# Hybrid flow-matching step on one core: VectorE's side work in the recurrent mixer regrouped, its output double-buffered, and the output projections split into fp32r

## The reference

```
out = jnp.concatenate([c_out, d_out], axis=-1) @ w_out       # (384, 1024) @ (1024, 1024)
x = x + gate * out
```

```
sa = einsum(s, kk_t)
s  = s * w_t - sa (kk_t * a_t) + v_t k_t
o  = einsum(s, r_t)
```

## Time and profile before

| | us |
|---|---|
| median of 3 runs (lowest, highest) | 1813.3 (1811.26, 1814.56) |
| the profiled execution, its own time | 1816.77 |
| span of the profile | 1815.1 |
| PE busy | 1563.8 (86%) |
| PEld busy | 1229.5 (68%) |
| DVE busy | 1128.4 (62%) |
| ACT busy | 723.6 (40%) |
| POOL busy | 265.4 (15%) |

### The profile page before, as it was taken

The page is one execution under the profiler, slowest core; times in us unless marked ns, Lnnn a source line. Parts: engine busy times, 40 slices in busy tenths (PEclk is TensorE's granted clock), DMA queues, the critical chain, the costliest instruction groups (busy, mean ns, idle before and its releaser), DMA issues. The chain is left out here.

```text
span 1815.1 us, 33539 instructions
## 1 busy us (share of the span) xinstructions
PE 1563.8 (86%) x13261; PEld 1229.5 (68%) x13261; DVE 1128.4 (62%) x1495; ACT 723.6 (40%) x1101; POOL 265.4 (15%) x276
## 2 busy tenths in 40 slices
PE   4779989799999987789898888868589999999982
PEld 1456665399999974476676767753468888888871
DVE  1158761279877612585856767641268889888884
ACT  3112222242332311441423415210267777877763
POOL 3400000142222110011101021001100111111111
PEclk8898997899999967899998989879589999999996
DMA  8794543088766204111010000020668999999984
GB/s 306 222 315 139 177 137 92 4 260 262 252 205 201 93 1 130 53 30 39 8 44 24 23 5 3 4 81 20 265 266 338 385 378 372 369 369 370 370 318 164
DMA packets 157576, 321.96 MB, mean 177 GB/s; under 512 B 13187, under 2 KB 104661, under 8 KB 151317
## 3 DMA queue, kind: packets, MB, share of 16 engines
q1 hardware_dynamic: 129750, 201.32, 31.0%
q0 software_dynamic: 26416, 114.28, 18.4%
q10 hardware_dynamic: 1296, 4.72, 0.6%
HBM read 299.15 MB, written 24.25 MB: 178 GB/s over the span
## 5 line engine op out<-in xcount | busy, mean ns | idle before, releaser
L2657 DVE TENSOR_TENSOR gate_up_low<-expert_gate_up,gate_up_high 128x1408 fp32r<-128x1408 f32 x147 | 231.5, 1622 | 17.9 <-ACT gate_up_high L2579 17.7
L2579 ACT ACTIVATE gate_up_high<-expert_gate_up 128x1408 fp32r<-128x1408 f32 x147 | 197.7, 1374 | 29.4 <-PE banks L2475 20.6
L2473 PE MATMUL banks<-gate_up_high,gathered_high 128*128 128x512 f32 (+1 forms) x432 | 165.9, 384 | 9.2 <-DVE gate_up_low L2657 9.2
L2475 PE MATMUL banks<-gate_up_high,gathered_low 128*128 128x512 f32 (+1 forms) x432 | 163.7, 379 | 0.0
L2474 PE MATMUL banks<-gate_up_low,gathered_high 128*128 128x512 f32 (+1 forms) x432 | 163.4, 378 | 0.0
L2653 DVE TENSOR_TENSOR down_low<-expert_down,down_high 128x1024 fp32r<-128x1024 f32 x99 | 118.7, 1223 | 51.5 <-ACT down_high L2572 51.2
L2572 ACT ACTIVATE down_high<-expert_down 128x1024 fp32r<-128x1024 f32 x99 | 102.2, 1052 | 75.6 <-PE banks L2475 61.2
L1137 DVE SCALAR_TENSOR_TENSOR mod_sums<-next_mod_w,silu_cond,mod_sums 128x2048 f32<-128x2048 f32 x48 | 125.4, 2659 | 7.0 <-DMA mod_sums<-in_mod_b 7.0
L1013 PE MATMUL banks<-ffn_in_high,gate_up_w_high 128*128 128x384 f32 x352 | 118.8, 337 | 5.0 <-DVE ffn_in_low L1118 4.1
L1015 PE MATMUL banks<-ffn_in_high,gate_up_w_low 128*128 128x384 f32 x352 | 118.4, 336 | 0.0
L1014 PE MATMUL banks<-ffn_in_low,gate_up_w_high 128*128 128x384 f32 x352 | 118.3, 336 | 0.0
(11 more groups left out here) (379 smaller groups left out, 3247.4 us busy)
## 6 DMA issues: line engine op xcount, KB each, us to landing
expert_gate_up<-in_moe_w_up SPq DMA_DIRECT2D x76, 704.0 KB, 8.0
expert_gate_up<-in_moe_w_gate SPq DMA_DIRECT2D x76, 704.0 KB, 7.8
expert_down<-in_moe_w_down POOLq DMA_DIRECT2D x99, 512.0 KB, 5.6
next_mod_w<-in_mod_w POOLq DMA_DIRECT2D x24, 1024.0 KB, 5.2
late_w<-in_mod_w POOLq DMA_DIRECT2D x16, 1024.0 KB, 5.2
gate_up_w<-in_ffn_w_gate SPq DMA_DIRECT2D x22, 512.0 KB, 6.1
gate_up_w<-in_ffn_w_up SPq DMA_DIRECT2D x22, 512.0 KB, 5.7
normed_by_channel<-in_ffn_w_down SPq DMA_DIRECT2D x22, 512.0 KB, 6.5
```

The source lines that it names most:

```text
L2473: nc.tensor.matmul(out, a[0], b[0], start=first, stop=False)
L2475: return nc.tensor.matmul(out, a[1], b[0], start=False, stop=last)
L2579: nc.scalar.activation(WH[:, u % SPLIT, :], raw[:, u % RAW, :], ACT.Copy).then_inc(high, 1)
L2657: v.tensor_tensor(WL[:, u % SPLIT, :], raw[:, u % RAW, :], WH[:, u % SPLIT, :], ALU.subtract).then_inc(low, 1)
```

## The change

Two functions are edited, and they have nothing to do with each other.

In `rwkv`, VectorE's side work gets other places. The log sums, `after_own` and one half of the reciprocal of `key_norm` move between the `xm` and the `up` step of a level; `out_norm` and `finished` move behind the chain; `keys` move behind the last level, and the four products of `operands` and the three steps of `shifted_values` into the gaps of the chain. The addition into `scan_out` now comes ahead of the masks of the first tile of pair j+1. `scan_out` gets two buffers, and ScalarE waits for pair j-2 in place of j-1.

In `mixed`, k becomes the outer loop: for each k ScalarE rounds one row block of weights (128 by 1024) and one of inputs (128 by 384), VectorE takes the differences, and TensorE runs 18 fp32r matmuls (3 for each of the 6 units). All six units end in the pass of the last k. The gated result goes through 2 buffers, the space of the first weight block, in place of 6.

```diff
 def mixed(R, l, ahead):
...
-        Y = sb(f"gated{l}", [P, 6, BANK])
-        done, gated = R.sem(f"mixed_done{l}"), R.sem(f"mixed_gated{l}")
+        MH, ML = sb(f"mixed_high{l}", [P, OUT_SPLIT, TOK], F32R), sb(f"mixed_low{l}", [P, OUT_SPLIT, TOK], F32R)
+        Y = W[:, 0, :].rearrange("p (u n) -> p u n", u=2)
+        WH, WL = sb(f"w_out_high{l}", [P, OUT_SPLIT, D], F32R), sb(f"w_out_low{l}", [P, OUT_SPLIT, D], F32R)
...
             def _(pe):
-                for t in range(TT):
-                    for h in range(2):
-                        for k in range(KT):
-                            if t == 0 and h == 0 and k % 2 == 0:
-                                pe.wait_ge(loaded[k // 2], 16)
-                            mm = nc.tensor.matmul(R.B[2 * t + h][:, :], R.MT[:, k, t * P:(t + 1) * P], W[:, k, h * BANK:(h + 1) * BANK],
-                                                  start=(k == 0), stop=(k == KT - 1))
-                        mm.then_inc(done, 1)
+                for k in range(KT):
+                    s = k % OUT_SPLIT
+                    pe.wait_ge(w_low, k + 1)
+                    pe.wait_ge(m_low, k + 1)
+                    for u, (t, h) in enumerate(units):
+                        tok, cols = slice(t * P, (t + 1) * P), slice(h * BANK, (h + 1) * BANK)
+                        nc.tensor.matmul(R.B[u][:, :], MH[:, s, tok], WH[:, s, cols], start=(k == 0), stop=False)
+                        nc.tensor.matmul(R.B[u][:, :], MH[:, s, tok], WL[:, s, cols], start=False, stop=False)
+                        mm = nc.tensor.matmul(R.B[u][:, :], ML[:, s, tok], WH[:, s, cols], start=False, stop=(k == KT - 1))
...
             def _(act):
+                for k in range(KT):
+                    act.wait_ge(loaded[k // 2], 16)
+                    if k >= OUT_SPLIT:
+                        act.wait_ge(w_used, k - OUT_SPLIT + 1)
+                    nc.scalar.activation(WH[:, k % OUT_SPLIT, :], W[:, k, :], ACT.Copy).then_inc(w_high, 1)
+                    nc.scalar.activation(MH[:, k % OUT_SPLIT, :], R.MT[:, k, :], ACT.Copy).then_inc(m_high, 1)
...
             def _(dve):
+                for k in range(KT):
+                    dve.wait_ge(w_high, k + 1)
+                    nc.vector.tensor_tensor(WL[:, k % OUT_SPLIT, :], W[:, k, :], WH[:, k % OUT_SPLIT, :], ALU.subtract).then_inc(w_low, 1)
+                    dve.wait_ge(m_high, k + 1)
+                    nc.vector.tensor_tensor(ML[:, k % OUT_SPLIT, :], R.MT[:, k, :], MH[:, k % OUT_SPLIT, :], ALU.subtract).then_inc(m_low, 1)
+                for u, (t, h) in enumerate(units):
                     dve.wait_ge(done, u + 1)
+                    if u >= 2:
+                        dve.wait_ge(added, u - 1)
...
 def rwkv(R):
...
-                    if j:
-                        act.wait_ge(dve_done, dve_at(f"yn.{j - 1}"))
+                    if j >= 2:
+                        act.wait_ge(dve_done, dve_at(f"yn.{j - 2}"))
...
+                def in_level(l, x, j):
+                    if (l, x) == (0, "up"):
+                        log_sum(j, 0)
+                    elif (l, x) == (1, "xm"):
+                        log_sum(j, 1)
+                    elif (l, x) == (1, "up"):
+                        before_own(j)
+                    elif (l, x) == (2, "xm"):
+                        after_own(j)
+                    elif (l, x) == (2, "up"):
+                        backward(j)
+                    elif l == 3:
+                        key_norm(j, 0 if x == "xm" else 1)
+                    elif (l, x) == (4, "up"):
+                        keys(j)
...
+                def between(gap, j):
+                    if gap == 1:
+                        operand(j, 0)
+                        operand(j, 1)
+                    elif gap in (2, 3):
+                        operand(j, gap)
+                    elif 4 <= gap < 7:
+                        shifted_values(j, gap - 4)
...
                     chains(j)
-                    if more:
-                        shifted_values(j + 1)
-                        first_inverse(0, j + 1)
+                    if j:
+                        out_norm(j - 1)
+                        finished(j - 1)
                     dve.wait_ge(pe_done, pe_at(f"out.{j}"))
                     dve.wait_ge(act_done, act_at(f"vu.{j}"))
-                    v.tensor_tensor(OS[:, :], OS[:, :], B[6][:, 0:TOK], ALU.add).then_inc(dve_done, dve_inc(f"os.{j}"))
+                    v.tensor_tensor(OSs[:, j % 2, :], OSs[:, j % 2, :], B[6][:, 0:TOK], ALU.add).then_inc(dve_done, dve_inc(f"os.{j}"))
+                    if more:
+                        first_inverse(0, j + 1)
                     dve.wait_ge(pe_done, pe_at(f"mean.{j}"))
```

152 lines of the change are left out of this document (85 added, 67 removed).

## The result

The changed kernel takes **1768.6 us** (median of 4 runs, 1765.4 to 1770.1), the kernel before on the same chip 1812.3 (4 runs, 1809.6 to 1814.6): a ratio of 0.9757, 95% interval 0.9737 to 0.9778, or 43.7 us less. The forecast was 1774.4, the range 1761 to 1791. The profiled execution after took 1765.4 us with a span of 1763.4, where 1815.1 stood before.

A forecast was written before the change was run, and what follows sets the result against it. It took the scan as bound by hand-overs between engines and what delays them, the projections by TensorE's work. 33.2 - 7.7 + 7.5 + 5.9 = 38.9 us off 1813.3 gave 1774.4 us, range 1761 to 1791.

The forecast's parts named there:

- One sign of being wrong: Projections: the prediction called itself wrong if fp32r products were spaced by more than 0.23 us past the first 3 us.
- Levels: The scan's levels, six pairs: VectorE's side work moved under waits gains 33.2 us, at 29.4 us per pair with side work.
- 0.9 (`after_own`, now between the two steps): Level 2: `after_own` between masked product and additions costs its whole 0.9 us, within 5.1 for the level.
- The 0.2 for hand-overs: Levels: an allowance of 0.2 us for hand-overs within the 29.4 us of each pair with side work.
- Chain: From the first u step on: the products and shifted v moved there cost 7.7 us, 3.0 plus 4.7 in pair 4.
- The delay of 1.5 in pair 0: Chain of pair 0: `beta` and `k_grown`, 2.8 us, in a wait of 1.30 for the second u step delay it 1.5.
- the cover of 2.32: Chains of pairs 1 to 3: a 2.32 us wait for the second u step covers `beta` and `k_grown`, leaving 0.5 each.
- Behind the chain: Behind the chain: adding into `scan_out` ahead of the masks gains 1.5 us in each of pairs 0 to 4, 7.5 in all.
- Projections: The two output projections: splitting them by k gains 1.7 us in layer 0 and 4.2 in layer 1, 5.9 in all.
- the full collision with GpSimd: Chain: GpSimd's work holds `beta` and `k_grown` to 2.57 us each, 11.7 more in five pairs, 1786 us; chance 0.17.
- a clock that falls in the levels: Levels: idle TensorE drops its clock, 2.4 us per level; all 25 give 1834, chance 0.04; a few 1780 to 1794, 0.10.
- The rule of the Trainium skill: Chain: the VectorE and GpSimd port lock makes `beta` and `k_grown` wait for GpSimd operations; gain some 3.5 us smaller, 1778.

The follow-up runs named there:

- waits_only: The changed kernel with the levels' side work one slot earlier, so nothing stands between the two steps of levels 2 and 3: 1762.6 us.
- masks_first: The changed kernel with the first tile's masks and inverse back ahead of the addition into `scan_out`: 1775.8 us.
- spread_out: The changed kernel with side work one slot earlier, chain products spread singly, the shifted v behind `finished` and 32 idle ScalarE activations per projection: 1753.6 us.
- gpsimd_later: The changed kernel with GpSimd's turn started behind the last of the chain's four products, in place of behind `neg_kk_a`: 1764.4 us.
- products_ahead: The changed kernel with the chain's four products back between `keys` and the first u step: 1794.5 us.

## Why the prediction was right, and where its sizes were off

The mechanism of the main term was right: time was lost where VectorE's side work stood between hand-overs, and comes back where it stands under waits. Most of the signs came: level 2 to the first u step 16.5 us ("near 17"), `beta` and `k_grown` 2.70 together (2.8), the projections 42.3 and 42.7, the last addition 8.2 behind the first gated product. One sign of being wrong came as well: fp32r products were spaced by more than 0.23 us past the first 3 us. That the total was within 5 us is in part luck. The scan gave 11.6 us more than its terms, the projections and the experts 7.5 less, and these two misses cancel in the main. Term by term:

- **Levels, 37.5 for 33.2.** The step "0.9 (`after_own`, now between the two steps)" and the same for 1.3 of the reciprocal counted whole lengths; a part is given back by the additions behind them, and `waits_only` measured 1.4 for the two in place of 2.2. The 0.2 for hand-overs was not needed either. That is 0.9 a pair, all of the difference in pairs 0 to 4. The halves of the reciprocal took 1.34 and 1.35, as assumed (1.3).
- **Chain, +4.0 for +7.7.** The delay of 1.5 in pair 0 came out as 1.39, but by another sum. Where the prediction put it, between the first s step and the second u step, it is 1.10. The first s step is 0.76 later, a term that the prediction doesn't have: before, VectorE came to the first u step so late that the s step followed at once (the row below, behind the u step at 823.15), and now it waits for TensorE (947.05 above has that wait in pair 2). Behind the second u step 0.47 is won back. In pairs 1 to 3 the step that failed is the cover of 2.32: that wait stood in a chain whose granted clock had fallen to 0.50, and with the clock at 1.00 it went away. At the full clock the cover is pair 0's 1.30; the delay is 1.4 there too, and the clock gives back 1.6 (15.23 for 13.65). The prediction had the clock as a risk of the levels and did not look for it in the chain. Pair 4's chain, 11.85, was forecast near 13: the new work in it lasted 5.7 us, not 6.3, and 2.5 of it was covered, not 1.6.

```profile
824.41 1.01 DVE L2092 SCALAR_TENSOR_TENSOR states<-states,chunk_decay,banks 128x64 f32<-128x64 f32 x4
```

- **Behind the chain, 11.1 for 7.5.** The order was sized rightly (6.8 measured, as the difference from `masks_first`). The other 4.3 goes with the granted clock, which the prediction didn't look for here either: 2.4 in pair 0, 0.4 to 0.7 in pairs 1 to 3, 0.1 in pair 4. Both traces of the old mixer with the new projections show such a long pair too, pair 1 (27.20), with the clock at 0.50 for the same 7 us. It isn't the shifted v, which no longer stands there: `spread_out` has it back behind the chain, and the stretch stays at 23.20. The double buffer, which the prediction counts as taking a wait of ScalarE's away, gave nothing: with one buffer there is no such wait at the new place either.
- **Projections, 4.6 for 5.9,** and 6.5 for the split alone with the stall out of the way. The spacing of the products at the full clock was right (0.227). At the start it was 0.43 until 4.35 us in layer 0 and 4.0 in layer 1, not for 3 us: summed over the products that cost 1.7 and 2.1 us in place of the 1.3 taken, most of the 1.3 that is missing.
- **The experts, +6.2 for nothing.** No step had it: the prediction put code that the change doesn't touch at nothing, and the stall on ScalarE's queue came with the longer program. It took away what the split gained, so that the total, 43.7 for 38.9, comes from the mixer alone.

Of the rivals, the full collision with GpSimd did not come (`k_grown` 1.75, not 2.57), nor a clock that falls in the levels. The rule of the Trainium skill that was weighed ("SBUF — State Buffer", section "SBUF: two separate sides") puts the sum at 1778; the hold-up it describes is there, as `gpsimd_later` shows, but `beta` and `k_grown` lose 0.8 to it in all and not the 1.6 of that sum. In `products_ahead`, where both stand beside GpSimd's first operations, they lose 3.3: how much depends on which operations meet.

## What to carry to other kernels

In a chain of hand-overs an operation that fits under the wait for another engine costs nothing, and the same operation between two dependent steps cost a good half of its length here. Where the operation leaves TensorE idle, a lower clock may follow, as in the chain of pair 1 before the change; so before a wait is counted as cover, look at the granted clock in it. When a stage gets shorter and the whole does not, compare the stretches of untouched code: a longer instruction stream on one engine can move a stall to a place where the others wait for it, and a few idle instructions tell that cause from contention. Do not size a move by the durations at its old place alone: beside GpSimd the same operations took 2.05 for 0.62 and 1.55 for 0.42.
